# Expert outputs weighted on ScalarE and added into stored residual rows by an accumulating scatter

## The reference

```python
weights = p_g[:, None] * jax.nn.softmax(top_vals, axis=-1)
...
def expert_block(args):
    xblk, e = args
    hdn = jax.nn.silu(xblk @ w_gate[e]) * (xblk @ w_up[e])
    return hdn @ w_down[e]
...
out = jnp.zeros((T + 1, D), yb.dtype).at[row_tok].add(yb * row_w[:, None].astype(yb.dtype))
...
h = layer_norm(DEEPNORM_ALPHA * h + y, *ln2[i])
```

## Time and profile before

| | us |
|---|---|
| median of 3 runs | 1186.28 (1185.05 to 1187.26) |
| time of the profiled execution | 1181.73 |
| its span, first to last instruction | 1179.8 |
| PE busy | 1072.1 (91%) |
| DVE busy | 804.7 (68%) |
| ACT busy | 619.1 (52%) |
| POOL (GpSimd) busy | 210.8 (18%) |

### The profile page before, as it was taken

One profiled execution on the slowest core, in us unless ns is written; L12 is line 12 of the kernel. 1 busy time (PEld: TensorE's weight loads), 2 busy tenths in 40 slices (PEclk: granted clock), 3 DMA queues, 4 the chain that ended last, 5 costly groups with the idle time before them and its releaser, 6 DMA issues.

```text
span 1179.8 us, 15389 instructions
## 1 busy us (share of the span) xinstructions
PE 1072.1 (91%) x5279; PEld 885.9 (75%) x5279; DVE 804.7 (68%) x1132; ACT 619.1 (52%) x665; POOL 210.8 (18%) x188
## 2 busy tenths in 40 slices
PE   6999999999999998949999999999999999999600
PEld 5878889678888786837788888888888888888500
DVE  3301223125456787778999898998998998998288
ACT  4311313213334420035878878878878878877511
POOL 3000112000000000011314323223223233232100
PEclk9999999999999999978999999999999999999955
DMA  7523313401211422157999999999999999998672
GB/s 246 180 94 117 116 44 125 125 18 36 72 38 57 176 90 72 55 189 282 414 359 364 398 383 382 404 387 382 392 369 380 391 378 380 402 379 311 229 307 106
DMA packets 64848, 284.09 MB, mean 241 GB/s; under 512 B 16125, under 2 KB 16125, under 8 KB 39205
## 3 DMA queue, kind: packets, MB, share of 16 engines
q1 hardware_dynamic: 51808, 254.14, 56.8%
q0 software_dynamic: 11840, 25.19, 5.8%
q10 hardware_dynamic: 1156, 4.20, 0.9%
HBM read 266.66 MB, written 33.55 MB: 254 GB/s over the span
## 4 chain that ended last, share of the span: by engine, by line
PE 82%; DVE 9%; DMA 4%; DVEq 2%; issue 2%; ACT 1%; SPq 1%; POOLq 0%; ACTq 0%
PE bank L1388 23%; PE bank L1390 23%; PE bank L1389 23%; PE bank L1729 2%; DVE wlo L1295 2%; PE bank L1759 1%; PE bank L1580 1%; PE bank L1582 1%; PE bank L1585 1%; PE bank L1629 1%; DVE hh L1366 1%; DVE yy L1372 1%; DMA hh<-h_rows 1%; DMA raw_up<-l_w_up 1%; PE bank L1540 1%
## 5 line engine op out<-in xcount | busy, mean ns | idle before, releaser
L1388 PE MATMUL bank<-whi,xghi 128*128 128x512 f32 x512 | 203.7, 398 | 1.4 <-DVE xglo L1304 1.4
L1390 PE MATMUL bank<-whi,xglo 128*128 128x512 f32 x512 | 201.0, 393 | 0.0
L1389 PE MATMUL bank<-wlo,xghi 128*128 128x512 f32 x512 | 200.3, 391 | 0.0
L1295 DVE TENSOR_TENSOR wlo<-raw_down,whi 128x2048 fp32r<-128x2048 f32 x64 | 146.3, 2292 | 34.1 <-ACT whi L767 34.1
L1388 PE MATMUL bank<-whi,xhi 128*128 128x512 f32 (+1 forms) x400 | 163.7, 409 | 2.9 <-ACT vext L686 1.6
L1389 PE MATMUL bank<-wlo,xhi 128*128 128x512 f32 (+1 forms) x400 | 158.6, 396 | 0.0
L1390 PE MATMUL bank<-whi,xlo 128*128 128x512 f32 (+1 forms) x400 | 158.2, 396 | 0.0
L1295 DVE TENSOR_TENSOR wlo<-raw,whi 128x2048 fp32r<-128x2048 f32 x64 | 146.0, 2289 | 3.5 <-ACT whi L767 2.2
L1295 DVE TENSOR_TENSOR wlo<-raw_up,whi 128x2048 fp32r<-128x2048 f32 x64 | 146.1, 2285 | 1.8 <-ACT whi L767 1.8
L767 ACT ACTIVATE whi<-raw_up 128x2048 fp32r<-128x2048 f32 x64 | 122.4, 1914 | 33.2 <-PE bank L1390 23.9
L767 ACT ACTIVATE whi<-raw_down 128x2048 fp32r<-128x2048 f32 x64 | 122.5, 1913 | 28.0 <-PE bank L1390 22.9
(11 more groups left out here) (300 smaller groups left out, 1599.1 us busy)
## 6 DMA issues: line engine op xcount, KB each, us to landing
raw<-l_w_gate SPq DMA_DIRECT2D x64, 1024.0 KB, 8.0
raw_up<-l_w_up SPq DMA_DIRECT2D x64, 1024.0 KB, 7.8
raw_down<-l_w_down SPq DMA_DIRECT2D x64, 1024.0 KB, 8.2
raw<-l_w_in SPq DMA_DIRECT2D x5, 2048.0 KB, 10.8
yy<-expert_rows SPq DMA_DIRECT2D x8, 1024.0 KB, 11.8
xt<-hcat SPq DMA_DIRECT2D x8, 512.0 KB, 3.4
o_rows<-stage POOLq DMA_DIRECT2D x16, 256.0 KB, 2.6
qkT<-qk_rows SPq DMA_DIRECT2D x16, 256.0 KB, 3.8
```

Source lines behind the costliest of these rows:

```text
L1295: tt(wlo[k][:, halves(p)], raw_e[k][:, halves(p)], whi[k][:, halves(p)].bitcast(F32), ALU.subtract).then_inc(e_lo[k], 1)
L1388: t.matmul(out, lh, rh, start=first, stop=False)
L1389: t.matmul(out, lh, rl, start=False, stop=False)
L1390: return t.matmul(out, ll, rh, start=False, stop=last)
```

## The change

`expert_rows` is gone. In its place is `sum_rows`, 1024 + 128 rows. ACT's queue stores each tile of `h1t` twice, to `h1_rows` and to `sum_rows`. The expert weights, divided by ALPHA, are computed before the loop begins (the exponentials on ACT before the second half of item 1's gate weights), and GpSimd stores them to a DRAM array `slot_weights`, one number for each of the 2048 expert rows. For each item GpSimd gathers the 128 weights of its slots into a column `wcol`, and ACT multiplies by it in `y_out`. The scatter then adds `yt` to the rows of `sum_rows` (`compute_op=ALU.add`); free slots go to 128 spare rows instead of being dropped, so all 128 rows move. Two accumulating scatters must not be in flight together, so scatter j waits until scatter j - 1 has landed, with one semaphore for all.

The tail loads one row for each token, 512 KB a tile, after the last scatter. LayerNorm does not mind the missing factor ALPHA but for EPS, which becomes EPS / ALPHA^2. DVE takes the mean of tile 0 with bn_stats; for tiles 1 to 7 ACT sums the row in a pass of its own, then the squares. The Newton chain runs twice, for four tiles each, instead of four times.

```diff
-    ys = nc.dram_tensor("expert_rows", (2 * T, D), F32).ap()
+    acc = nc.dram_tensor("sum_rows", (T + P, D), F32).ap()
+    w_dram = nc.dram_tensor("slot_weights", (2 * T, 1), F32).ap()
...
+        sp.wait_ge(N["scattered"], pairs_m1 * 32 + 32)
         for n in range(NT):
-            t0 = n * P
-            sp.dma_start(hh[n], h1_dram[t0:t0 + P, :]).then_inc(h_landed[n], 16)
-        for s in range(2):
-            sp.wait_ge(scattered[s], pairs_m1 * 16 + 16)
-        for n in range(NT):
-            t0 = n * P
-            sp.dma_start(yy[n].rearrange("p a d -> p (a d)"), ys[2 * t0:2 * (t0 + P), :].rearrange("(p a) d -> p (a d)", a=2)).then_inc(y_landed[n], 16)
+            sp.dma_start(hh[n], acc[n * P:(n + 1) * P, :]).then_inc(acc_landed[n], 16)
...
-        def scatter(j, b):
+        def slot_weights(j, b):
             jj = slice(j, j + 1) if isinstance(j, int) else bass.ds(j, 1)
-            wait(pool, scattered[b], (j - b) * 8)
+            wait(pool, N["scattered"], j * 16 - 16)
+            wait(pool, w_gathered[b], (j - b) * 8)
+            g.tensor_copy(aix[b][:], sumrow[:, jj])
             g.tensor_copy(dix[b][:], dstrow[:, jj]).then_inc(dix_ready[b], 2)
-            wait(pool, N["y_cp"], j * 2 + 2)
             wait(pool, dix_ready[b], j - b + 2)
             pool.sem_inc(N["pool_passed"], 1)
-            g.indirect_dma_start(ys[0:2 * T, :], bass.IndirectOffsetOnAxis(dix[b][:].bitcast(U32), 0), yt[b][:], None,
-                                 bounds_check=last_row, oob_is_err=False).then_inc(scattered[b], 16)
-
+            g.indirect_dma_start(wcol[b][:], None, w_dram[0:2 * T, :], bass.IndirectOffsetOnAxis(dix[b][:].bitcast(U32), 0),
+                                 bounds_check=last_row, oob_is_err=False).then_inc(w_gathered[b], 16)
+
+        def scatter(j, b):
+            wait(pool, N["scattered"], j * 16)
+            wait(pool, N["y_cp"], j * 2 + 2)
+            pool.sem_inc(N["pool_passed"], 1)
+            g.indirect_dma_start(acc[0:T + P, :], bass.IndirectOffsetOnAxis(aix[b][:].bitcast(U32), 0), yt[b][:], None,
+                                 bounds_check=last_sum, oob_is_err=True, compute_op=ALU.add).then_inc(N["scattered"], 16)
...
+        pool.wait_ge(N["w_done"], 1)
+        g.dma_start(w_dram.rearrange("(n p k) o -> p n (k o)", p=P, k=2), wts[:]).then_inc(N["w_stored"], 16)
...
+        pool.wait_ge(N["w_stored"], 16)
+        pool.wait_ge(N["routed_n"], 1)
+        slot_weights(0, 0)
         for j in range(6):
             scatter(j, j % 2)
+            slot_weights(j + 1, (j + 1) % 2)
             gather(4 + j, j % 2)
...
+            act.dma_start(acc[i * P:(i + 1) * P, :], h1t[i % 2][:]).then_inc(acc_stored[i % 2], 16)
...
             if q == 0:
-                wait(act, scattered[b], (j - b) * 8)
+                wait(act, N["scattered"], j * 16 - 16)
+                wait(act, w_gathered[b], (j - b) * 8 + 16)
             wait(act, N["y2_mm"], j * 3 + (1 + 2 * q))
-            a.activation(yt[b][:, q * 512:(q + 1) * 512], ps[5 + q][:], ACT.Copy).then_inc(N["y_cp"], 1)
+            a.activation(yt[b][:, q * 512:(q + 1) * 512], ps[5 + q][:], ACT.Copy, scale=wcol[b][:, 0:1]).then_inc(N["y_cp"], 1)
...
         xg_hi(1, 1)
+        act.wait_ge(N["w_arg"], 1)
+        a.activation(r_g4[:], r_g4[:], ACT.Exp)
+        a.activation(r_s[:, 1, :], r_s[:, 0, :], ACT.Exp).then_inc(N["w_exp"], 1)
         hi_expert(1, 0, 1)
...
         lo_expert(1, 0, 1)
+        expert_weights()
...
+        row_sum(1)
+        for n in range(2, NT):
+            row_sum(n)
+            squares(n - 1)
+        squares(NT - 1)
...
+        first_stats()
+        for n in range(1, 4):
+            mean(n)
+        spread(range(0, 4))
+        for n in range(4):
+            final(n)
+            mean(n + 4)
+        spread(range(4, NT))
+        for n in range(4, NT):
+            final(n)
```

More of the change, by code:

```diff
@@ L133, in build @@
     r_thr = at("r_thr", [P, 8])
+    r_spare = at("r_spare", [P, 1])
     tokrow = at("tokrow", [P, ITEMS], I32)
@@ L198, in over @@
         return nc.alloc_sbuf_tensor_at(name, list(shape), dt, offset=offsets[t])
+    sumrow = over("garg", "sumrow", [P, ITEMS], I32)
     hres = [over(f"qkT{i}", f"hres{i}", [P, D]) for i in range(2)]
@@ L220, in build @@
     dix = [at(f"dix{i}", [P, 1], I32) for i in range(2)]
+    aix = [at(f"aix{i}", [P, 1], I32) for i in range(2)]
+    wcol = [at(f"wcol{i}", [P, 1]) for i in range(2)]
     cursor[0] = offsets["cm_rows"]
@@ L585, in _ @@
             scatter(pairs_m2 * 2 + j, j % 2)
+            if j < 3:
+                slot_weights(pairs_m2 * 2 + (j + 1), (j + 1) % 2)
     @block.scalar
@@ L804, in _ @@
                 hi_expert(0, k, p)
+        for b in range(2):
+            act.wait_ge(acc_stored[b], 16 * (NT // 2))
         xg_hi(0, 0)
@@ L848, in _, with row_sum, squares @@
         item(1, 1)
[L849 to L862, removed]
+        pairs_m2 = act.value_load(npm1[0:1, 2:3], min_val=NE // 2 - 2, max_val=ITEMS // 2 - 2)
+        with act.Fori(0, pairs_m2) as i:
+            item(i * 2 + 2, 0)
+            item(i * 2 + 3, 1)
+        item(pairs_m2 * 2 + 2, 0, ahead=1)
+        item(pairs_m2 * 2 + 3, 1, ahead=0)
+        def row_sum(n):
+            act.wait_ge(acc_landed[n], 16)
+            a.activation(yy[n][:, 1, :], hh[n], ACT.Copy, accum_out=fsum[:, n:n + 1]).then_inc(N["f_sum"], 1)
+        def squares(n):
+            act.wait_ge(N["f_mean"], n)
+            a.activation(yy[n][:, 1, :], hh[n], ACT.Square, bias=fneg[:, n:n + 1], accum_out=fsq[:, n:n + 1]).then_inc(N["f_sq"], 1)
+        row_sum(1)
[3 more added lines that the diff above has]
+        squares(NT - 1)
     @block.vector
@@ L1332, in item @@
             hidden_lo(j)
-            if not ahead:
-                expert_weights()
             if isinstance(j, int) and j == 3:
@@ L1355, in _, with centred, first_stats @@
         item(pairs_m1 * 2 + 1, 1, ahead=0)
-        for m in range(0, NT, PAIR):
-            pair = slice(m, m + PAIR)
-            for n in range(m, m + PAIR):
-                dve.wait_ge(N["f_scaled"], n + 1)
-                dve.wait_ge(y_landed[n], 16)
-                stt(hh[n], yy[n][:, 0, :], wts[:, n, 0:1], hh[n], ALU.mult, ALU.add)
+        def centred(n):
+            stt(yy[n][:, 0, :], hh[n], fneg[:, n:n + 1], g2, ALU.add, ALU.mult)
+        def first_stats():
+            dve.wait_ge(acc_landed[0], 16)
+            for q in range(2):
+                v.bn_stats(lst[:, q, :], hh[0][:, q * 512:(q + 1) * 512])
@@ L1364, in _ @@
             dve.drain()
-            for n in range(m, m + PAIR):
-                stt(hh[n], yy[n][:, 1, :], wts[:, n, 1:2], hh[n], ALU.mult, ALU.add, accum_out=fsum[:, n:n + 1])
+            v.bn_aggr(lmv[:, 0, 0:2], lst[:].rearrange("p a b -> p (a b)"))
             dve.drain()
-            ts(fneg[:, pair], fsum[:, pair], -1.0 / D, None, ALU.mult).then_inc(N["f_sum"], 1)
+            ts(fneg[:, 0:1], lmv[:, 0, 0:1], -1.0, None, ALU.mult)
+            ts(fsq[:, 0:1], lmv[:, 0, 1:2], float(D), None, ALU.mult)
@@ new lines, in first_stats, with mean, spread @@
+            centred(0)
+        def mean(n):
+            dve.wait_ge(N["f_sum"], n)
+            ts(fneg[:, n:n + 1], fsum[:, n:n + 1], -1.0 / D, None, ALU.mult).then_inc(N["f_mean"], 1)
+            dve.drain()
+            centred(n)
+        def spread(tiles):
+            cols = slice(tiles.start, tiles.stop)
+            dve.wait_ge(N["f_sq"], tiles.stop - 1)
+            ts(fvar[:, cols], fsq[:, cols], 1.0 / D, EPS / ALPHA ** 2, ALU.mult, ALU.add)
+            dve.drain()
+            newton_rsqrt(frs[:, cols], fvar[:, cols], ftmp[:, cols])
@@ L1382, in _, with final @@
+        def final(n):
+            stt(yy[n][:, 0, :], yy[n][:, 0, :], frs[:, n:n + 1], b2, ALU.mult, ALU.add).then_inc(N["f_out"], 1)
+        first_stats()
[8 more added lines that the diff above has]
+            final(n)
     @block.tensor
```

61 lines of the change are left out of this document (28 added, 33 removed).

## The result

The changed kernel takes 1193.74 us (1190.81 to 1198.17) against 1186.28 before: a ratio of 1.007, with a 95% interval of 1.0049 to 1.0091. It is slower by 0.7%, against a forecast of 1197.0. The profiled execution has a span of 1189.5 us, 9.7 more than before.

What follows compares the result with a forecast made beforehand. The prediction took the expert loop as bound by PE, with DMA right behind. Tail -23.2, start +8 and loop +26 gave +10.8 us, added to the median 1186.28 for 1197 us; range 1170 to 1232.

Steps and rivals of the forecast that it cites:

- The case that was given 0.46: Expert loop: DMA's load or GpSimd's weight-gather chain adds 0.7 to 1.8 us an item, total 1189 to 1218; chance 0.46.
- Tail, -23.2 predicted: Last stage: fewer loads, no scalings or weighted sums, so the end comes 23.2 us earlier; bounds -18 to -26.
- The 1.0 us that the dropped scalings should give: Last item: ghi no longer waits for four ACT scalings and starts 1.0 us earlier.
- Start, +8 predicted: Loop start: ACT's first expert row waits for weights stored to and gathered from DRAM, +8 us; bounds 0 and +11.
- DMA is full here: Loop start: with DMA full, the weights' store was taken to land after 8.5 us.
- Loop, +1.0 an item for 26 items predicted: Items 4 to 29: the scatter's added DMA load costs +1.0 us an item, +26 in all; bounds 0 and +2.2 each.
- The double read: Loop scatter: reading the destination costs as much again, 2.88 us for 0.72, +2.16 of DMA work an item.
- The other sum, by shares: Loop: DMA's work goes from 17.6 us to 18.4 to 20.2, so an item takes 18.2 to 20.0 us.
- loop unmoved: Rival: DMA has room, the loop grows 0 to 0.5 us an item, total 1171 to 1184, faster; chance 0.34.
- long circle: Rival: the scatter lands late and GpSimd's chain paces items at 19.1 to 21 us, total 1207 to 1254; chance 0.12.
- -0.7 to +1.3: Loop: ACT waiting for the weight gather, and the next scatter for ACT, binds by -0.7 to +1.3 us an item.
- The median: Whole kernel: the difference of +10.8 us was added to the runs' median, 4.5 us above the profiled time, giving 1197.

Runs made afterwards that it cites:

- the fastest kernel: Changed kernel with padding dropped, slots interleaved, weights stored as 128 runs of 64 bytes and worked out some 10 us earlier: 1163.43 us, ratio 0.9824 to before.
- the kernel with 64-byte pieces: Changed kernel with padding dropped and slots interleaved (1168.63 us), plus weights stored as 128 pieces of 64 bytes instead of 1024 of 8: 1170.13 us.
- the kernel with the spread slots: Changed kernel, all 128 rows still added, with only the order of slots interleaved over both halves of the partitions: 1178.57 us, ratio 0.9949 to before.

## Why the prediction was right or wrong

The sum was +10.8 against the profiled execution and +9.7 was measured. The case that was given 0.46, the loop slowed by DMA to 18.5 to 19.5 us an item, came about, and the mechanism named for it, the read of the destination on full DMA engines, is the one that the runs show, with an uneven load of the engines on top that the prediction did not have. Two of the three terms, the start and the loop, came out near their numbers in part by luck.

**Tail, -23.2 predicted, -21.8 and -0.6 for the last items measured.** Right in nearly every step. The chain and DVE's timeline of the changed kernel:

```profile
1146.54 6.17 DMA sum_rows<-yt,aix
...
1156.05 1.29 DVE L1397 BATCH_NORM_STATS2 lst<-hh 128x6 f32<-128x512 f32 x2 [18.46 <-DMA hh<-sum_rows]
...
1181.24 4.87 DVE L1421 SCALAR_TENSOR_TENSOR yy<-yy,frs,ln_gb 128x1024 f32<-128x1024 f32 x4
```

The scatter lands after 6.2 us, 5.1 was predicted. DVE starts 3.3 us later (3.7), and from there 33.4 us pass to the end (33.8). The 1.0 us that the dropped scalings should give came and was lost again: `ghi` starts right behind the transposes, at 1136.27, and PE waits 1.41 us for what follows from it where it waited 2.39 before, but from 1138 to 1142 us the clock stood at 0.57 (window in the section on the result). In the fastest kernel it stayed at 1.00 and the last item takes 13.8 us, for 15.0 in the changed kernel and 14.7 before. Why the clock fell there is open: PE's waits around it are shorter than before, where it did not fall.

**Start, +8 predicted, +7.5 measured.** 0.8 of the 7.5 lies ahead of the loop. The column was there at 566.7, where 570 was named: the store's landing was right (8.5, measured 8.3), the gather's too long (9.3, measured 6.3). ACT's first `yt` half came 5.5 us later than before, not 8.8; what brings the sum back near 8 is that item 1 then took 1.9 us more, with PE idle and at half clock, for which the prediction had no term. That is luck. And the step "DMA is full here" reckoned with what the crowd does to the store, and not with what the store does to the crowd: the weights' loads fell to half their rate. The wait that I predicted is real, as the kernel with 64-byte pieces shows, but in the changed kernel more than half of it is hidden behind that stall.

**Loop, +1.0 an item for 26 items predicted, +24.5 measured.** The double read stands: 2.6 to 2.7 us for 128 rows, against 1.3 plain, where the prediction's upper bound had 2.88. By the records of single packets it is 327 ns for 159. The mis-sized step is the rate. I took 408 GB/s as between two rates held by all engines, and it gave +1.0; a more even load does better, 18.23, or +0.5 an item. The rest of the measured +1.2 in the steady part is that gathers load one half of the engines. I knew that padding moves nothing and did not ask on which partitions it lies. The other sum, by shares, took before's share of 0.993 for 17.6 us of work an item; 16.1 are what the table above has (14.7 and 1.44), and the rest is packets that wait. The +26 came out for +24.5 because a term short by 0.2 us an item met a slow part that began late, and that is luck as well. The first few items ran at 17.75: loads had to slip from landing after 7.8 us to landing after 14 before ACT waited.

**Rival "loop unmoved".** Its figure, 424 to 435 GB/s, was nearly right: by the table above the loads run at 428. It was wrong in spreading GpSimd's work evenly. The Trainium skill, "DMA: Bandwidth & Descriptors" (section "Where 436 GB/s comes from"), has 435 GB/s as the ceiling, and an item was an estimated 17.6 us by it; the kernel with the spread slots measures 18.23, as the packets that add are no quicker than 200 GB/s of rows.

**Rival "long circle" and the supporting term "-0.7 to +1.3".** Refuted: no wait of `yt` for the weight gather from 650 to 1100 us, and the same period without the wait. The weight gather landed after 7.8 us, not 8.0 to 10.7, and since the whole item is longer the circle has more room. It supported nothing.

**The median.** 1197.0 for 1193.74 measured. 1.1 us is the sum. The rest is that I added the distance of before's profiled time to its median, 4.5, and for the changed kernel that distance is 2.4.

## What to carry to other kernels

Where a DMA drops part of its rows, ask which partitions the rest lies on: a mean share over 16 engines says nothing when some of them get it all, and here an interleaved order of slots was worth 23 us where 64 rows are added and 15 in the changed kernel. A DMA that adds cost twice a plain one here, so move work into it only where the loads beside it have that much to spare on the fullest engines. When two delays start together at one place, taking one away shows only part of its price, or none; take both. And before two profiles are compared at one place, count from a common event just ahead of it: absolute times of the loop's start differ by some 3 us here for reasons that lie in the mixer.

## What the runs showed that I had not expected

- A store of 8 KB in 1024 pieces of 8 bytes halves the DMA rate of everything beside it for some 5 us (213 GB/s for 419, at a share of 0.99); in 128 pieces of 64 bytes it lands after 5.4 us instead of 8.3 and the rate stays at 428. That small pieces cost is in the Trainium skill, "DMA: Bandwidth & Descriptors" (section "Why small descriptors are slow (HBM only)"), which counts a fixed overhead for each; the trace agrees in direction, and that the other queues pay for it is what these runs add.
- An accumulating scatter of 128 rows of 4 KB holds all engines for 2.6 us (200 GB/s), and the last one, alone on the DMA, lands after 6.2 us, for 3.38 without the add. With some 64 rows it is 3.2 plain and 5.55 adding, with the rows over both halves.
- PE idle for 6.2 us was followed by a granted clock of 0.50 for the next five, so a stall at one place is paid for again behind it: from item 0 to item 1 it is 20.8 us here, and 18.7 in the fastest kernel, where PE waits 1.34 us at that place.
